# Attention, joins and query projections of the second layer, tile by tile between the expert rounds

## The reference

```python
q = (xb @ w_q).reshape(blk, 8, 256)            # 8 retrieval heads
v1, i1 = top_k(q[..., :128] . k1, 16); v2, i2 = top_k(q[..., 128:] . k2, 16)
e = top 16 of the 256 sums v1 + v2             # experts i1 * 128 + i2
gate = softmax(sv); act = gelu(einsum('thkd,td->thk', u[e], xb))
y = einsum('thk,thkd->td', gate * act, v[e])
```

## Time and profile before

| what | us |
|---|---|
| median of 3 runs | 2556.7 |
| lowest, highest | 2556.15, 2585.53 |
| the profiled execution, its own time | 2551.78 |
| its span in the trace | 2550.0 |
| busy: PE, DVE, POOL, ACT | 1281.6, 1208.0, 1225.6, 262.5 |

### The profile page before, as it was taken

The page is one execution under the profiler, slowest core; times in us unless marked ns, Lnnn a source line. Parts: engine busy times, 40 slices in busy tenths (PEclk is TensorE's granted clock), DMA queues, the critical chain, the costliest instruction groups (busy, mean ns, idle before and its releaser), DMA issues. The chain is left out here.

```text
span 2550.0 us, 19617 instructions
## 1 busy us (share of the span) xinstructions
PE 1281.6 (50%) x5982; PEld 632.0 (25%) x5982; DVE 1208.0 (47%) x3011; ACT 262.5 (10%) x601; POOL 1225.6 (48%) x1104
## 2 busy tenths in 40 slices
PE   7888786242245555566435778861101232324453
PEld 6676355011011111122001555550000000000010
DVE  3555457898644444432000342388787565552000
ACT  3333111000011111111000211110000000000000
POOL 1111033766765555574553000346557777776554
PEclk9898798575676777767777878985555555656776
DMA  7341247797877878899888000577668999999987
GB/s 230 109 124 39 108 182 279 282 344 269 307 274 273 285 283 304 306 357 364 296 310 289 29 0 1 215 269 264 244 232 310 346 365 355 375 350 332 307 303 261
DMA packets 234832, 648.55 MB, mean 254 GB/s; under 512 B 20937, under 2 KB 92130, under 8 KB 232050
## 3 DMA queue, kind: packets, MB, share of 16 engines
q0 software_dynamic: 152064, 553.72, 59.5%
q1 hardware_dynamic: 82674, 93.70, 10.9%
HBM read 641.23 MB, written 6.10 MB: 254 GB/s over the span
## 5 line engine op out<-in xcount | busy, mean ns | idle before, releaser
L818 POOL DMA_INDIRECT arena<-in_peer_u,idx x512 | 609.0, 1189 | 462.3 <-DVE arena L1158 233.3
L1158 DVE SCALAR_TENSOR_TENSOR arena<-arena,x 128x1024 f32<-128x1024 f32 x512 | 611.2, 1224 | 315.5 <-DMA arena<-in_peer_u,idx 307.3
L923 PE MATMUL bank<-arena,wbig 128*32 128x512 f32 x2048 | 412.2, 949 | 649.8 <-DMA arena<-in_peer_v,idxT 635.8
L818 POOL DMA_INDIRECT arena<-in_peer_v,idxT x512 | 542.3, 1059 | 296.0 <-issue 145.2
L923 PEld LDWEIGHTS bank<-arena,wbig 128*32 128x32 f32 x2048 | 82.2, 149 | 940.5 <-issue 938.3
L664 DVE BATCH_NORM_STATS2 stats<-bank 128x6 f32<-128x512 f32 (+1 forms) x24 | 15.5, 683 | 497.6 <-PEq L998 401.5
L840 POOL MEMSET g_all<- 128x1024 f32 x2 | 1.9, 952 | 283.7 <-PE bank L645 229.4
L880 PE MATMUL bank<-xT,arena 128*128 128x264 f32 (+2 forms) x576 | 127.8, 385 | 6.1 <-ACT xT L627 2.9
L313 PE MATMUL bank<-xT,arena 128*128 128x264 f32 x512 | 116.9, 390 | 1.0 <-DMA arena<-in_hgrn_w_in 1.0
L880 PEld LDWEIGHTS bank<-xT,arena 128*128 128x128 f32 x576 | 106.8, 208 | 23.6 <-issue 3.5
L460 POOL TENSOR_TENSOR scratch<-scratch 128x128 f32<-128x128 f32 x16 | 7.0, 440 | 201.0 <-DVEq L509 201.0
(11 more groups left out here) (374 smaller groups left out, 1819.5 us busy)
## 6 DMA issues: line engine op xcount, KB each, us to landing
arena<-in_hgrn_w_in SPq DMA_DIRECT2D x32, 512.0 KB, 6.1
arena<-in_peer_w_q SPq DMA_DIRECT2D x16, 1024.0 KB, 10.0
scratch<-in_cache_kv SPq DMA_DIRECT2D x96, 144.0 KB
arena<-in_peer_u,idx POOLq DMA_INDIRECT x512
arena<-in_peer_v,idxT POOLq DMA_INDIRECT x512
arena<-in_mla_w_uq SPq DMA_DIRECT2D x2, 2304.0 KB
g_all<-in_cache_kv SPq DMA_DIRECT2D x32, 144.0 KB
arena<-in_state_hgrn SPq DMA_DIRECT2D x8, 512.0 KB, 6.0
```

Source lines behind the costliest of these rows:

```text
L818: pool.indirect_dma_start(out=dst, out_offset=None, in_=table, in_offset=bass.IndirectOffsetOnAxis(ap=rows, axis=0)).then_inc(done, 16)
L923: mm = pe.matmul(ybank(t, c, P)[32 * j:32 * j + 32, :], wspread[:, j, m, :], vring[:, (n + j) % RING, 512 * c:512 * c + 512], start=False, ...
L1158: dve.scalar_tensor_tensor(uring[:, r, :], uring[:, r, :], 1.0, x[:, t, :], ALU.mult, ALU.mult, accum_out=dots[t][:, TOPK * h + k:TOPK * h ...
```

## The change

Attention of the prompt, the output join, the norm and the query projections of layer 1 are no longer done for both tiles together between the layers.

- **Tile 0** (its norm after the experts, down projection, latents, four groups, output join, norm, the projections of heads 0 and 1) is spread over PE's queue behind v rounds 1 to 29 of tile 1 of layer 0. It attends to tile 0 alone, as the causal mask allows. DVE and ACT do their parts in that time, and DVE routes head 0.
- **Tile 1** is spread over the `u` dots of tile 0 in layer 1 (`tile0_last`), beside the projections of heads 2 to 7 of tile 0 (`pe_peer_last`). Keys and values of tile 0 are computed again for it.
- The projections of heads 2 to 7 of tile 1 and the samples stand behind the v rounds of tile 0 in layer 1.
- The **samples' experts** in layer 1 move from tile 0's dots to the `v` stage of tile 1: their `u` rows behind 32 of the tile's `v` rows, their `v` rows in the middle.
- Each tile has its own operands in its ring's place, so several weights are loaded twice: the down projection, `w_uq`, `w_ukv`, `w_o` (each in two halves) and the query weights (16 loads of one head for layer 1, two slots, started by ACT). The norm weights are loaded anew whenever the order needs the other pair.
- `pT` and `kfT` are now copied by ACT alone.

```diff
@@ PE, layer 0, tile 1
             for m in range(32):
-                add_round(1, m)
-                if l == 0 and m < 4:
-                    pe_decode_end(pe, m)
+                add_round(pe, 0, 1, m)
+                if m == 0:
+                    pe_turn_probs(pe, NS - 1)
+                elif m == 1:
+                    pe_weigh_pages(pe, NS - 1)
+                    pe_turn(pe, 3, 0)
+                elif m == 2:
+                    pe_decode_fold(pe)
+                elif m == 3:
+                    pe_down(pe, 0)
+                elif m == 4:
+                    pe_decode_out(pe)
+                elif m == 5:
+                    pe_latents(pe, 0)
+                elif m == 6:
+                    pe_queries(pe, 0, 0)
+                elif m < 20:
+                    g, j = divmod(m - 7, 3)
+                    if j == 0:
+                        if g:
+                            pe_mix(pe, 0, g - 1)
+                        if g < NG:
+                            pe_keys(pe, 0, g)
+                    elif j == 1:
+                        pe_scores(pe, 0, g)
+                        if g < NG - 1:
+                            pe_queries(pe, 0, g + 1)
+                    else:
+                        pe_probs(pe, 0, g)
+                elif m == 20:
+                    pe_join_turn(pe, 1, 0)
+                elif m in (21, 22):
+                    pe_join_half(pe, 1, 0, m - 21)
...
+                elif m == 26:
+                    pe_project(pe, 1, 0, 1, 0, P)
+                    pe_score(pe, 1, 0, 0)
...
@@ PE, layer 1
+        def pe_peer_last(pe):
+            ask(2)
+            pe_turn(pe, 3, 1)
+            pe_score(pe, 1, 2, 0)
+            pe_down(pe, 1)
+            ask(3)
+            pe_latents(pe, 1)
+            pe_score(pe, 1, 3, 0)
+            pe_queries(pe, 1, 0)
+            pe_sample_out(pe)
+            for g in range(NG):
+                pe_keys(pe, 1, g)
+                if g < 3:
+                    ask(4 + g)
+                pe_scores(pe, 1, g)
+                if g < NG - 1:
+                    pe_queries(pe, 1, g + 1)
+                if g < 3:
+                    pe_score(pe, 1, 4 + g, 0)
+                else:
+                    ask(7)
+                    pe_score(pe, 1, 7, 0)
+                pe_probs(pe, 1, g)
+                pe_mix(pe, 1, g)
+            pe_join(pe, 1, 1)
+            pe_join(pe, 1, 2)
...
+            for m in range(32):
+                if m == 16:
+                    add_samples(pe, 1)
+                add_round(pe, 1, 1, m)
@@ DVE, layer 1
+            def tile0_last():
+                dve_ln(dve, 1, (1,))
+                route(1, 0)
+                dot(0, 0, range(8))
+                norm_latents(dve, 1)
+                dot(0, 0, range(8, TOPK))
+                route(2, 0)
+                own_queries(dve, 1, 0)
+                for g in range(NG):
+                    dot(g + 1, 0, range(8))
+                    softmax(dve, 1, g)
+                    if g < NG - 1:
+                        own_queries(dve, 1, g + 1)
+                    dot(g + 1, 0, range(8, TOPK))
+                    route(g + 3, 0)
+                    take_mixed(dve, 1, g)
+                dve.sem_inc(mixed, 1)
+                dot(5, 0, range(8))
+                dve_ln(dve, 2, (1,))
+                route(7, 0)
+                tile_routed(0)
+                dot(5, 0, range(8, TOPK))
+                dve_ln(dve, 2, (2,))
+                dot(6, 0)
+                take_indices(0)
+                route(0, 1)
+                normalise(0)
+                dot(7, 0)
+                dotted()
+                route(1, 1)
+                weigh(0)
+                place_weights(0)
@@ POOL, layer 1
+                pool.wait_ge(stored, 64)
+                for h in range(HH):
+                    pool.wait_ge(idx_ready, 2 * HH + h + 1)
+                    for k in range(TOPK):
+                        u(0, TOPK * h + k)
...
+                for i in range(P // 4):
+                    v(1, i)
+                pool.wait_ge(sidx_ready, 2)
+                for h in range(HH):
+                    u(2, h)
+                for i in range(P // 4, P // 2):
+                    v(1, i)
+                for h in range(HH):
+                    v(2, h)
+                for i in range(P // 2, P):
+                    v(1, i)
@@ SP, between the layers
             sp.wait_ge(dots_ready, 3)
-            sp.wait_ge(po_made, NS)
-            load_down(sp)
+            load_up(0)
+            sp.wait_ge(po_made, NS - 1)
+            load_down(sp, 0)
+            sp.wait_ge(x_ready, 3 + normed(1, 0))
+            sp_ln(sp, 2)
...
+            sp.wait_ge(v_free, NROW)
+            load_down(sp, 1)
```

More of the change, by code:

```diff
@@ L964, in pe_peer, with seed, turn_indices @@
             mm.then_inc(repack_ready, 1)
-            add_samples()
+        def seed(pe, t):
+            nt = TILES[t][1]
+            for c in range(2):
+                pe.matmul(ybank(t, c, nt), cst[0:nt, C_AID:C_AID + nt], x[0:nt, t, 512 * c:512 * c + 512],
+                          start=True, stop=False, skip_group_check=True)
+        def turn_indices(pe, l, t):
+            pe.wait_ge(ef_ready, 2 * l + t + 1)
+            if t:
+                pe.wait_ge(wdiag_ready, 2 * l + 1)
+            pe.transpose(bank[(7, 5)[l]][:, 256:384], ef[t].rearrange("p h k -> p (h k)"), ident).then_inc(efT_ready, 1)
@@ L967, in pe_peer, with pe_first @@
             pe.sem_inc(y_ready, 1)
[L968 to L974 removed]
+        def pe_first(pe):
+            pe.wait_ge(turn_taken, turned(2, 0))
+            for s in range(2):
+                pe_project(pe, 0, 0, s, 0, P)
+            pe_score(pe, 0, 0, 0)
+            pe.wait_ge(rs_taken, score_step(0, 0, 0) + 1)
@@ new lines, in pe_peer @@
+        def pe_peer(pe):
+            pe.wait_ge(turn_taken, turned(2, 2))
+            for s in range(2):
+                pe_project(pe, 0, 0, s, P, NT, True)
+            pe_score(pe, 0, 0, 1)
+            for h in range(1, HH):
+                for s in range(2):
+                    pe_project(pe, 0, h, s, 0, NT)
+                for t in range(2):
+                    pe_score(pe, 0, h, t)
+            pe_sample_score(pe, 0)
+            pe_spread_samples(pe, 0)
+            seed(pe, 2)
+            pe_repack(pe, 0)
+            add_samples(pe, 0)
+            pe_sample_query(pe)
+            pe.wait_ge(sidx_ready, 1)
+            turn_indices(pe, 0, 0)
+            seed(pe, 0)
+            turn_weights(pe, 0, 0)
+            pe.wait_ge(wdiag_ready, 1)
@@ new lines, in pe_keys @@
+        def pe_keys(pe, t, g):
+            n = NG * t + g
+            if g == 0:
+                pe.wait_ge(olT_taken if t == 0 else os_out, 1)
+            for a in range(t + 1):
+                for c in range(2):
+                    mm = pe.matmul(mla_bank[t][1 + a][:, :], ckvT[:, c, a * P:(a + 1) * P], w_ukv[:, c, 512 * g:512 * (g + 1)],
+                                   start=(c == 0), stop=(c == 1))
+            mm.then_inc(kv_ready, 1)
+            pe.wait_ge(qrot_ready, n + 2)
+            for h in range(HG):
+                mm = pe.transpose(mla_bank[t][3][0:QD, h * P:(h + 1) * P], qs[t][:, h, :], ident)
+            mm.then_inc(qT_ready, 1)
+            pe.wait_ge(kv_taken, n + 1)
+            for a in range(t + 1):
+                for h in range(HG):
+                    mm = pe.transpose(mla_bank[t][4 + a][0:QD, h * P:(h + 1) * P], kf[t][:, a, h, :], ident)
+            mm.then_inc(kT_ready, 1)
@@ new lines, in pe_scores @@
+        def pe_scores(pe, t, g):
+            n = NG * t + g
+            pe.wait_ge(qT_taken, n + 2)
+            pe.wait_ge(kT_taken, n + 1)
+            for h in range(HG):
+                if t == 0:
+                    mm = pe.matmul(mla_bank[0][3][:, h * P:(h + 1) * P], qfT[0][:, h, :], kfT[0][:, 0, h, :], start=True, stop=True)
+                else:
+                    mm = pe.matmul(mla_bank[1][3 + h // 2][:, (h % 2) * 256:(h % 2) * 256 + 256], qfT[1][:, h, :],
+                                   kfT[1][:, :, h, :], start=True, stop=True)
+            mm.then_inc(s_ready, 1)
```

1081 lines of the change are left out of this document (601 added, 480 removed).

## The result

The changed kernel takes 2389.75 us (median of 4 runs, 2360.98 to 2399.5) against 2563.24 us of the kernel before (4 runs). The ratio is **0.9272, 95% interval 0.9159 to 0.9385**: faster by 7%. It is the ratio of the means (2380.2 to 2567.0 us), without the changed kernel's slowest run, which fell in a slower state of the chip. The forecast was 2372. The profiled execution took 2385.25 us, its span 2383.4.

What follows compares the result with a forecast made beforehand. Each stretch had its own limit: A and D the 8-row ring, B DVE, C high DMA share with busy POOL. 1170 + 247 + 327 + 362 + 252 + 7.6 = 2366 us span, forecast 2372 us, range 2320 to 2440.

Steps and rivals of the forecast that it cites:

- B with the hole in it: From layer 0's last v round to tile 0's placed weights in layer 1: 568.3 us falls to 327, DVE leading.
- The hole: Between layer 0's last v gather and layer 1's first u gather: 253 us without gathers, to shrink below 20.
- the three terms of 30, 10 and 7 us: DVE's waits before tile 0's weights are placed: u rows 30, tile 1's output join 10, its first latents and scores 7.
- Term A: Tile 1's v rounds in layer 0: 221.7 us grows by 25 to 247, bounds -25 and +82.
- 22 for PE's chunks: Tile 1's v rounds, layer 0: tile 0's projection costs 6 us, join 6, four groups 2 each, head projections 2.
- 3 for the loads: Tile 1's v rounds, layer 0: some 13.7 MB more loads fit at 388 GB/s, costing 3 us.
- Rival 3: Better than summed: tile 1's layer 0 v rounds stay 222 us, u-row waits halve; 2322 us in all, chance 0.15.
- Term C: Layer 1, tile 1's u rows alternating with tile 0's v rows: 354.0 us grows by 8 to 362, bounds 350 and 375.
- Term D: Tile 1's v rounds in layer 1: the samples' 16 rows add 24 us to 228.4, giving 252.
- Attention of tile 0 paid in A: Tile 1's v rounds in layer 0: chunks wait in PE's in-order queue, +82 for +25; 2429 us, chance 0.15.
- Attention of tile 1 paid in B: Among tile 0's layer 1 dots: groups' chains are waited for, 88 us less the 5 counted; 2455 us, chance 0.12.
- Slower by long issues: POOL's queue: every gather issued at 1.98 + 0.30 us beside DVE work; 2689 us, chance 0.04.

Runs made afterwards that it cites:

- e10_finer_and_route: Changed kernel with tile 0's down projection in halves, its output join in quarters, and DVE's routing of head 7 ahead of tile 1's join norm: ratio 0.9197 to before.
- e11_best: Changed kernel with down projection in halves, join in quarters, later chunks re-placed, and head 7 routed ahead of tile 1's join norm: 2357.5 us against 2556.6, ratio 0.9224.
- e4_even_chunks: Changed kernel with tile 0's down projection in two halves, everything after it one round later, output join in quarters: ratio 0.9192 to the kernel before.
- the control: The changed kernel itself, unaltered, run again on a faster chip: 2284.11 us against 2466.97 for the kernel before, ratio 0.9265.
- e3_small_loads: Changed kernel with tile 0's w_o load cut to a quarter, tile 1's w_ukv and query weights of heads 0 to 3 to an eighth: ratio 0.9153 to before.
- bef_profile: The kernel before the change, unaltered, profiled once more on a faster chip: 2461.38 us, span 2459.6.

## Why the prediction was right

The time came out 18 us above the forecast and inside its own range. The profiled span is 2383.4 against a sum of 2366: 7 us of that lie ahead of the change, 10 in A, 9 in C, and B gives 8 back. The large term, B with the hole in it, was right for its reasons. That the total is within 1% also has some luck in it: A's price was taken too low and B's waits for u rows too high, and these errors cancel.

**The mechanism.** The hole is gone as foretold: the seam is 2.1 us wide, where under 20 was forecast. A ends at 1434 (forecast 1417). The weights of tile 0 are placed at 1753 (forecast 1744). DVE's waits in B after the change, to be read beside the earlier trace rows:

```profile
DVE stats L677 <- PEq L1105: 23.7, 1, 23.7
DVE arena L1419 <- DMA arena<-in_peer_u,idx: 14.5, 9, 3.3
DVE stats L677 <- PE bank L654: 11.4, 1, 11.4
DVE rstd L2218 <- ACTq L2081: 5.0, 1, 5.0
```

The first row is DVE out of work in A; it ends at 1438.30, 3.9 us after A's last round. The other three are the three terms of 30, 10 and 7 us: 14.5, 11.4 and 5.0. What is left, 318.6 - 30.9 - 3.9 = 284 us, is DVE's work with the small gaps between its instructions, where the sum said 280. So the work was counted right, and the waits for u rows at twice their size. B is 318.6 against 327. DVE is busy 84% of B, and the one wait near 10 us ahead of the join's norm is there.

**Term A is the step that was mis-sized.** Forecast +25, measured +35 here and +39 on the faster chips. The split was 22 for PE's chunks and 3 for the loads. The runs show 18 for 8.6 of the 13.7 MB of loads; in proportion all of them cost some 29, which is an estimate. Finer chunks in other places give back 5.7 (`e10_finer_and_route`) to 10.5 (`e11_best`), and the 18 of `e4_even_chunks` are in part work and gathers moved out of A. What the chunks cost in all was not measured. By this estimate the forecast had the larger part of the price on the wrong cause.

My 3 us rested on a rate: 83.8 MB at 388 GB/s take 216 us, so they "fit". The bytes were right (257.1 us x 331 GB/s = 85.1 MB). But A is a loop of a landing, a round and four issues, and a load beside the gathers makes the one landing late that the next round needs. The clearest place is behind the first half of `w_o`, 2 MB, which SP starts at 1218.61 in the control; `e3_small_loads` loads a quarter of it. The same round in the control, then in that run:

```profile
1231.61 3.64 PE L998 MATMUL bank<-arena,wbig 128*32 128x512 f32 x16 [9.54 <-DMA arena<-in_peer_v,idxT]
```

```profile
1224.36 3.37 PE L998 MATMUL bank<-arena,wbig 128*32 128x512 f32 x16 [3.75 <-DMA arena<-in_peer_v,idxT]
```

In the profile of the result the round at this place waits 7.67 us. Before the change the longest such wait in A was 7.0 (8.2 in `bef_profile`).

The chunks are the other cause. The timeline of PE in the profile of the result:

```profile
1203.94 9.57 PE L1914 MATMUL bank<-scratch,xT 128*128 128x288 f32 x32
...
1219.63 3.64 PE L998 MATMUL bank<-arena,wbig 128*32 128x512 f32 x16
...
1235.07 3.64 PE L998 MATMUL bank<-arena,wbig 128*32 128x512 f32 x16 [10.53 <-DMA arena<-in_peer_v,idxT]
```

The first line is a chunk of 9.57 us in one piece, longer than any wait of a round before the change. The two rounds behind it find their rows landed, and the next one waits 10.53 us. Loads are in this wait too: two query weights (ACT, 1217.10) and the 2 MB of `w_ukv` (SP, 1219.98) start just ahead of it. With the query weights cut to an eighth it is 8.81 us against 10.71 in the control. The longest wait, 11.70 us, follows the two halves of the join and the second load of `w_ukv`. With that load cut to an eighth it is still 10.04 us. In `e11_best`, with the load whole and the join in quarters, the round at this place waits 4.94 us. So this wait comes mostly of how the chunks stand. PE's and POOL's waits in A:

```profile
PE bank L998 <- DMA arena<-in_peer_v,idxT: 74.2, 16, 11.7
```

```profile
POOL arena L840 <- PE bank L998: 106.7, 23, 10.7
```

Rival 3 was right in one thing: of the 14 rounds in A that directly follow PE work 12 take 1.92 us. In all, 16 of the 32 rounds do, at a granted clock of 0.80 for the stretch; before it was 11, at 0.72. What this gave can't be told apart from the rest, and A grew all the same, since landings and chunks held the loop.

**Term C**, +8 for 4.2 MB of query weights, came out +19, and on a faster chip +2. The window holds 246 gathers where the kernel before had 239 and 238, since fewer of C's gathers are issued ahead of the placing. Per gather C takes 352.0 / 239 = 1.47 and 371.4 / 246 = 1.51 us on the chip of the result, 1.45 and 1.41 on the faster ones. POOL's waits in C tell the two sorts of chip apart: after the change on the first chip, then the control on a faster one.

```profile
POOL arena L840 <- issue: 71.3, 234, 0.3
POOL arena L840 <- remote: 19.2, 8, 3.0
POOL arena L840 <- DVE arena L1419: 7.2, 1, 7.2
```

```profile
POOL arena L840 <- issue: 74.4, 244, 0.3
POOL arena L840 <- PE bank L998: 1.5, 2, 0.8
```

"Remote" is a releaser that the trace cannot name. The kernel before has 7.1 us of such waits in C on the first chip, `e11_best` 18.5 on its chip, and the faster chips none. So 12 of the 19 us are waits of that kind; what ends them is open. That my 8 lies between the 2 and the 19 is luck: its reason (bytes of query weights) was not shown, for with them cut to an eighth, on a faster chip, C moved by less than it varies.

**Term D**, +24, came out +20.7, but the rows of the samples explain 8 to 10 of it. The sum was near for a reason that only half holds.

**The rivals.** Attention of tile 0 paid in A (+82): no, +35. Attention of tile 1 paid in B: no, none of the four softmaxes waits, and undoing the cover costs B 131 us. Slower by long issues: POOL's mean issue in C is 272.46 / 246 = 1.11 us, in A 123.58 / 128 = 0.97. Before the change it was 0.94 in A, with 7.3 us of DVE work there; with 39.8 us the issues are hardly longer. The Trainium skill, SBUF — State Buffer, section "SBUF: two separate sides", warns of such a lock; this case's traces show none that moves a stretch.

## What to carry to other kernels

Look first for the stage that is led by one engine while the others idle. Here the attention of tile 1 was hidden almost whole beside DVE's dots; the price was paid in A, which is a loop of latencies, and not in C, where the DMA share is highest. In a loop of landing, round and issue, cost a load by the landing that it delays, and not by whether its bytes fit under the peak rate. Put other work between the rounds in pieces shorter than the round's own wait, and give each wait for a long chain a piece of independent work of its own, as the routing ahead of the norm did.

## What was not expected of the hardware

- Chips differ by 4% for one kernel: 2461 and 2557 us. 74 us of the gap lie ahead of A. The traces of the slower chips have waits on releasers that cannot be named (18.5 us in C of `e11_best`), those of the faster ones none. The ratio of the changed kernel is the same on both (0.9265 and 0.9272); that of single stretches is not.
- C held 383 GB/s for 348 us at a DMA share of 0.99 in the control. The Trainium skill, DMA: Bandwidth & Descriptors, section "Specifications", gives about 358 GB/s as the HBM limit of a core. This trace does not agree: with one core at work the measurement is higher, and it decides. No run here has a second core at work. The window:

```profile
1676.30:2024.20 347.90, 146.63 (x745) 56.40 (x745) 210.07 (x491) 9.92 (x35) 272.34 (x246) 0.65 0.99 383
```
